# A token norm's sums, roots and reciprocals as nine columns instead of three packed strips

## The chip, the cores and the metric

The kernel runs on one core of a Trainium2 chip. The metric is the device time of one execution in microseconds (us), lower is better. TensorE (PE in the rows, its weight loads PEld) multiplies into PSUM, VectorE (DVE) and ScalarE (ACT) compute on tiles and move them out of PSUM, GpSimd (POOL) computes on SBUF only, and SyncE (SP) issues most of the transfers.

## The reference

One inference step of a trunk of two layers, for a prompt of 1024 tokens and for 8 samples of 8 tokens, with the same weights, all in float32. Layer 0 is a gated MLP, layer 1 ("the sparse layer") an attention in which a small indexer picks 256 keys for each query. Each layer is

```python
x <- x + W_out( mixer(rmsnorm(x, g)) * silu(z) )
x <- x + sigmoid(rmsnorm(x, g_pe) @ w_gate) * (p @ w_pe)

def rmsnorm(x, g):
    r = rsqrt(mean(x * x, axis=-1) + EPS)      # one number for each token
    return x * r * g
```

The work here is the first norm of layer 1: for each of 1088 tokens the sum of the squares of its 1024 features, a root, a reciprocal, and then the scaled `x` that goes into the projections of layer 1.

## The kernel before

`x` lies transposed in SBUF: `xT` is 128 partitions (features) by 8 tiles (k) by 1092 columns (64 sample tokens, 1024 prompt tokens, 4 columns of padding). All matrix products are made of three passes with float32r operands, a high and a low part of each side: `hhi`, `hlo` for the activations, `whi`, `wlo` for the weights. One unit is a product of a 1024 x 128 weight slab with all tokens; `full_unit` takes it in 8 steps over k, each of 9 matmuls with 364 columns (three column pieces, three passes), recorded at line 499, and each step waits for the low part of its tile k.

Each engine has its own program; semaphores alone join them. The order around the change is this:

- The end of layer 0's second half, the gate. For each feature tile TensorE makes a gate product (L499) and an embedding product (L2358); VectorE multiplies (L1599, L1603) and adds into `xT` (L1609); ScalarE makes the sigmoid (L1090); GpSimd squares the finished tile (L823) and adds it to `acc` (L824), for the first seven tiles.
- ScalarE squares the last tile into `sig` (`sparse_square`, L561).
- TensorE sums over the partitions (`strip_sums`, L570), by matmuls with ones: 32 columns of ones are the weights, 364 columns of squares move, and the three column pieces go to three strips of 32 PSUM partitions of bank 0. It does so for `acc`, waits for `sig`, and adds `sig`.
- ScalarE takes the root of 96 partitions by 364 columns (`strip_roots`, L576), VectorE the reciprocal (`strip_inverse`, L581).
- TensorE spreads the result back over all 128 partitions (`strip_spread`, L587): one row of ones is the weights, one row of reciprocals moves, from partitions 0, 32 and 64 into banks 5, 6, 7.
- Then the norm proper, for each k: VectorE scales `xT` by gain and reciprocal into `hfb` (L606), ScalarE rounds it to `hhi` (`norm_hi`, L592), VectorE subtracts for `hlo` (L612). There are two buffers of `hfb`. TensorE's first unit (U_IK, indexer keys) takes the tiles as they come.

ScalarE splits the next unit's weights (L482, `split_unit`) after the root, and GpSimd makes their low part (L487). SyncE waits for the count 2 of the norm's `sum` semaphore, loads the cosine and sine tables for the indexer (L727, L728) and goes on with weight slabs (L662).

A `Turn` gives each use of the norm the counts that its semaphores had before it; the turns are written out as tuples at the top of the kernel. For the sparse layer `sum` counts 2 in this kernel, one for the sums and one for the spread.

Of the kernel before, what the change touches and what calls it, by code (L numbers as in the profile page):

```python
# [22 lines left out]
ALU = mybir.AluOpType  # L23
ACT = mybir.ActivationFunctionType
AX = mybir.AxisListType

P = 128
D = 1024
KD = D // P
SEQ, DEC_B, DEC_T = 1024, 8, 8  # L30
NS = DEC_B * DEC_T
NT = NS + SEQ
TP = NT + 4
NC3 = TP // 3
# [17 lines left out]
BANK = 512  # L52
# [14 lines left out]
def tile_cols(j):  # L67

    return (0, NS) if j == 0 else (NS + CHUNK * (j - 1), CHUNK)
# [52 lines left out]
def hybrid_trunk(nc, x_prompt, x_sample, cache_k, cache_v, cache_ik, page_table, p_prompt, p_sample,  # L122
# [5 lines left out]
    with ctx:  # L128
# [23 lines left out]
        ident = fixed("ident", [P, P])  # L152
        ones = fixed("ones", [P, P])
        gains = fixed("gains", [P, NGAIN])
        gn = gains[:, 0:2 * KD].rearrange("p (l f) -> p l f", l=2)
# [3 lines left out]
        eps = fixed("eps", [P, 1])  # L159
        ss = fixed("ss", [P, 9])  # L160
        sv = fixed("sv", [P, 5])
        rv = fixed("rv", [P, 5])
        rx = fixed("rx", [P, 9])
# [5 lines left out]
        rbc = fixed("rbc", [P, TP])  # L169
# [52 lines left out]
        hhi = pl("hhi", [P, KD, TP], F32R)  # L222
        H1 = D0 + KD * TP * 4
        H2 = (END - KD * TP * 4) // 32 * 32
        hlo = nc.alloc_sbuf_tensor_at("hlo", [P, KD, TP], F32R, offset=H2)
# [11 lines left out]
        hfb = pl("hfb", [P, 2, TP])  # L237
# [87 lines left out]
        PS = ctx.enter_context(nc.psum_tensor("PS", [P, 8, BANK], F32))  # L325
        PSF = PS[:].rearrange("p b n -> p (b n)")
# [9 lines left out]
        def as3(ap):  # L336
# [9 lines left out]
        x_tr, x_sq, x_ev, x_rt, x_dg = (sem(n) for n in ("x_tr", "x_sq", "x_ev", "x_rt", "x_dg"))  # L346
# [5 lines left out]


        norm = {n: sem(f"norm_{n}") for n in ("sum", "rt", "hf", "hi", "lo")}
        turns = [Turn(norm, {"sum": (0, 2, 3, 6, 8)[t], "rt": (0, 0, 0, 3, 4)[t], "hf": KD * (0, 1, 2, 2, 3)[t],
                             "hi": KD * t, "lo": KD * t}) for t in range(5)]
        nA, nG, nB = turns[0:2], [turns[2], turns[4]], turns[3]

# [199 lines left out]
        def sparse_square(act):  # L558

            act.wait_ge(sG[0]["xup"], sG[0].at("xup", KD + 1))  # L560
            nc.scalar.activation(sig[:], xT[:, KD - 1, :], ACT.Square).then_inc(sq7, 1)  # L561

        def strip_sums(pe, s):

            pe.wait_ge(stat, 3)
            for part, squares in enumerate((acc, sig)):
                if part:
                    pe.wait_ge(sq7, 2)
                for c, (a, n) in enumerate(ALL_COLS):
                    mm = nc.tensor.matmul(PS[STRIP * c:STRIP * c + STRIP, 0, 0:n], ones[:, 0:STRIP], squares[:, a:a + n],  # L570
                                          start=part == 0, stop=part == 1)
            mm.then_inc(s["sum"], 1)

        def strip_roots(act, s):
            act.wait_ge(s["sum"], s.at("sum", 1))
            nc.scalar.activation(rbc[0:3 * STRIP, 0:NC3], PS[0:3 * STRIP, 0, 0:NC3], ACT.Sqrt, bias=eps[0:3 * STRIP],  # L576
                                 scale=1.0 / D).then_inc(s["rt"], 1)

        def strip_inverse(dve, s):
            dve.wait_ge(s["rt"], s.at("rt", 1))  # L580
            nc.vector.reciprocal(rbc[0:3 * STRIP, 0:NC3], rbc[0:3 * STRIP, 0:NC3]).then_inc(x_dg, 1)  # L581

        def strip_spread(pe, s):
            pe.wait_ge(x_dg, 4)
            for c, (a, n) in enumerate(ALL_COLS):
                row = slice(STRIP * c, STRIP * c + 1)
                mm = nc.tensor.matmul(PS[:, 5 + c, 0:n], ones[row, :], rbc[row, 0:n], start=True, stop=True)  # L587
            mm.then_inc(s["sum"], 1)

        def norm_hi(act, s, k, hi, hf):  # L590
            act.wait_ge(s["hf"], s.at("hf", k + 1))
            nc.scalar.activation(hi(k), hf(k), ACT.Copy).then_inc(s["hi"], 1)  # L592
# [22 lines left out]
        def norm_dve(dve, own, s, cols, *tile):  # L615
            a, n = cols[0][0], sum(c[1] for c in cols)
            if s in nA:
                dve.wait_ge(s["sum"], s.at("sum", 2))
            else:
                strip_inverse(dve, s)  # L620
                dve.wait_ge(s["sum"], s.at("sum", 2))
            for k in range(KD + 1):
                norm_tile(dve, s, k, a, n, *tile)

# [2 lines left out]
            return [(c0 + n // np_ * m, n // np_) for m in range(np_)]  # L627

        ALL_COLS = [(NC3 * c, NC3) for c in range(3)]
        STRIP = 32  # L630


        PIECES_P = [(kk, m, ((1, 2, 3), (0, 7, 3))[kk][m], NS * kk if m == 2 else 0, *(((NS, 512), (NS + 512, 512), (0, NS))[m]))
# [292 lines left out]
        def _(act):  # L926
            own = Tally(act, av)
# [44 lines left out]
            for g in range(2):  # L972
                c0, n, nch, has_s, np_ = GROUPS[g]
                h = n // np_
                s = sA[g]
# [134 lines left out]

            gate_act(0, False)

            sparse_square(act)
            strip_roots(act, nB)
            split_unit(U_IK + 1)
            for k in range(KD):
                norm_hi(act, nB, k, lambda k: hhi[:, k, :], lambda k: hfb[:, k % 2, :])

            def swap(dst, slot, size, scale, n=P):

# [272 lines left out]
            for f in range(KD):  # L1393
                act.wait_ge(oy["y"], f + 1)
                cols = slice(0, NS if f == 0 else TP)
# [10 lines left out]
        def _(dve):  # L1406
# [215 lines left out]
            def evac_out(f):  # L1622
# [3 lines left out]
                for m in range(3):  # L1626
# [4 lines left out]
                    else:  # L1631
# [1 line left out]

            gate_dve(0, False)

            norm_dve(dve, own, nB, ALL_COLS, lambda k: gn[:, 1, k:k + 1],
                     lambda k: hfb[:, k % 2, :], lambda k: hhi[:, k, :], lambda k: hlo[:, k, :], PS[:, 5:8, 0:NC3])

            def rotate(s, used, f, slot, dst, cs, sn, g):
                rotate_front(s, used, f, slot, cs, g)  # L1640
# [508 lines left out]
        def _(pe):  # L2149
# [258 lines left out]
                        within[i][1]()  # L2408
                mm.then_inc(w_used, 1)

            strip_sums(pe, nB)
            strip_spread(pe, nB)
            pe.wait_ge(sG[0]["t"], sG[0].at("t", KD + 1))
            def head_sum(n, rows, c):

# [391 lines left out]
```

## Time and profile before

| | us |
|---|---|
| median of 3 runs | 1891.24 |
| lowest, highest | 1890.42, 1893.8 |
| the profiled execution | 1889.96 |
| its span, first to last instruction | 1888.3 |
| TensorE busy | 1821.9 (96%) |
| VectorE busy | 889.5 (47%) |
| ScalarE busy | 796.0 (42%) |
| GpSimd busy | 617.8 (33%) |

All marks of time in the rows are microseconds from the start of the span. The profile's clock of TensorE (PEclk) is the granted share of 2.4 GHz, so 0.50 is 1.2 GHz. A float32 matmul that is not a transpose stands in the profile as two records, each with a weight load of its own; "x6" at the strip sums means three matmuls. The time of a record runs to the modelled end of a pipelined instruction, so records that follow each other overlap.

### The profile page before, as it was taken

The page shows a single profiled execution, that of the slowest core. Times are in us where ns is not written, and L with a number is a line of the kernel's source. Part 1 is how long each engine was busy: PE and PEld are TensorE (multiplying, and loading weights), DVE is VectorE, ACT ScalarE, POOL GpSimd, SP SyncE. Part 2 cuts the span into 40 slices and gives each one's busy share as a digit, 9 for nine tenths or more (in the row PEclk, how much of TensorE's full clock was granted, in tenths as well). Part 3 has the DMA queues.
Part 4 walks back from the last instruction along what each step waited for, and adds up shares of the span by engine and source line. Part 5 has one row for each costly group of instructions (what it writes and reads, how often), then busy time and mean ns, then how long its engine had stood idle before and what let it go on. Part 6 is the DMA issues. An engine that isn't in the chain of part 4 may idle for free.

```text
span 1888.3 us, 30009 instructions
## 1 busy us (share of the span) xinstructions
PE 1821.9 (96%) x10858; PEld 1616.9 (86%) x10858; DVE 889.5 (47%) x1647; ACT 796.0 (42%) x1186; POOL 617.8 (33%) x363
## 2 busy tenths in 40 slices
PE   8999999999999999999979989999999999899998
PEld 6889999999888888889969559999987776699997
DVE  3173333332124443142255877688778745612423
ACT  6243333222243333242235775477876554402211
POOL 4353333355444444644422131121121002254221
PEclk9999999999999999999989889999999999899999
DMA  5232222223333223331122110311242005521111
GB/s 195 78 90 78 78 67 78 78 78 89 91 99 89 83 84 89 90 112 45 33 106 80 31 57 23 93 44 58 92 130 63 1 1 207 197 92 43 46 58 48
DMA packets 203063, 150.81 MB, mean 80 GB/s; under 512 B 16626, under 2 KB 188450, under 8 KB 202594
## 3 DMA queue, kind: packets, MB, share of 16 engines
q1 hardware_dynamic: 188482, 127.88, 22.8%
q0 software_dynamic: 4272, 12.38, 2.0%
q10 hardware_dynamic: 10224, 9.46, 1.5%
q8 instruction: 48, 0.79, 0.2%
q14 instruction: 37, 0.30, 0.0%
HBM read 133.24 MB, written 16.43 MB: 79 GB/s over the span
## 4 chain that ended last, share of the span: by engine, by line
PE 88%; DVE 5%; issue 2%; ACT 2%; DMA 1%; POOL 1%; SPq 0%; ACTq 0%; DVEq 0%; POOLq 0%
PE PS L499 60%; PE PS L2217 10%; PE PS L2648 3%; PE PS L2618 3%; PE PS L2358 3%; PE PS L2483 2%; PE PS L2288 2%; PE PS L2664 1%; PE PS L2582 1%; DVE qT L2046 1%; DVE hlo L612 0%; POOL wlo L487 0%; PE PS L2504 0%; PE PS L2684 0%; PE PS L2636 0%
## 5 line engine op out<-in xcount | busy, mean ns | idle before, releaser
L487 POOL TENSOR_TENSOR wlo<-wraw,whi 128x1024 fp32r<-128x1024 f32 x177 | 434.8, 2457 | 752.1 <-ACT whi L482 751.6
L482 ACT ACTIVATE whi<-wraw 128x1024 fp32r<-128x1024 f32 x177 | 187.0, 1056 | 427.6 <-PE PS L499 314.0
L499 PE MATMUL PS<-hhi,whi 128*128 128x364 f32 x1176 | 270.3, 339 | 11.3 <-DVE hlo L612 7.1
L499 PE MATMUL PS<-hlo,whi 128*128 128x364 f32 x1176 | 262.5, 332 | 0.0
L499 PE MATMUL PS<-hhi,wlo 128*128 128x364 f32 x1176 | 261.0, 331 | 0.0
L499 PEld LDWEIGHTS PS<-hhi,whi 128*128 128x128 f32 x1176 | 204.2, 191 | 18.8 <-issue 12.0
L499 PE MATMUL PS<-hhi_g,whi 128*128 128x288 f32 (+1 forms) x768 | 214.5, 333 | 2.2 <-DVE v_raw L1488 1.8
L499 PE MATMUL PS<-hhi_g,wlo 128*128 128x288 f32 (+1 forms) x768 | 210.9, 329 | 0.0
L499 PE MATMUL PS<-hlo_g,whi 128*128 128x288 f32 (+1 forms) x768 | 210.5, 328 | 0.0
L499 PEld LDWEIGHTS PS<-hlo,whi 128*128 128x128 f32 x1176 | 206.9, 190 | 0.0
L499 PEld LDWEIGHTS PS<-hhi,wlo 128*128 128x128 f32 x1176 | 206.7, 190 | 0.0
L499 PEld LDWEIGHTS PS<-hhi_g,whi 128*128 128x128 f32 x768 | 130.2, 189 | 14.9 <-issue 2.3
L499 PEld LDWEIGHTS PS<-hhi_g,wlo 128*128 128x128 f32 x768 | 130.2, 188 | 11.7
L499 PEld LDWEIGHTS PS<-hlo_g,whi 128*128 128x128 f32 x768 | 130.8, 189 | 10.9
L1547 DVE TENSOR_TENSOR t2a<-PS,szt 128x576 f32<-128x576 f32 (+1 forms) x32 | 23.2, 725 | 206.2 <-PE PS L499 206.2
L499 PE MATMUL PS<-yhi,whi 128*128 128x288 f32 (+1 forms) x384 | 106.2, 331 | 0.0
L499 PE MATMUL PS<-ylo,whi 128*128 128x288 f32 (+1 forms) x384 | 105.2, 328 | 0.0
L499 PE MATMUL PS<-yhi,wlo 128*128 128x288 f32 (+1 forms) x384 | 104.9, 328 | 0.0
L1784 DVE TENSOR_SCALAR_CACHE_REDUCE acc<-sc,thr 128x384 bf16<-128x384 f32 (+1 forms) x124 | 100.7, 812 | 4.1
L1090 ACT ACTIVATE sig<-hfb 128x1092 f32<-128x1092 f32 x16 | 17.9, 1118 | 177.0 <-DVE hfb L1599 177.0
L1581 DVE TENSOR_TENSOR xT<-PS,xT 128x576 f32<-128x576 f32 (+1 forms) x16 | 11.6, 725 | 143.0 <-PE PS L499 143.0
L1171 ACT ACTIVATE acc<-sc,thr 128x896 bf16<-128x896 f32 (+1 forms) x62 | 67.8, 1093 | 20.9 <-DVE thr L1770 19.8
(421 smaller groups left out, 3106.6 us busy)
## 6 DMA issues: line engine op xcount, KB each, us to landing
wraw<-in_w_in_a_dram SPq DMA_DIRECT2D x96, 512.0 KB, 3.9
wraw<-in_w_out_a_dram SPq DMA_DIRECT2D x32, 512.0 KB, 4.0
wraw<-in_w_in_b_dram SPq DMA_DIRECT2D x25, 512.0 KB, 3.8
wraw<-in_w_pe_gate_dram SPq DMA_DIRECT2D x16, 512.0 KB, 4.0
kpg<-in_cache_k_dram SPq DMA_DIRECT2D x64, 128.0 KB, 2.9
vpg<-in_cache_v_dram POOLq DMA_DIRECT2D x48, 128.0 KB, 2.9
xs<-xT SPq DMA_DIRECT2D x1, 4368.0 KB, 12.6
xT<-xs SPq DMA_DIRECT2D x1, 4368.0 KB, 13.3
```

Of the source, the lines that this page charges most:

```text
L482: nc.scalar.activation(whi[par][:], wraw[par][:], ACT.Copy).then_inc(w_hi, 1)
L487: nc.gpsimd.tensor_tensor(wlo[par][:], wraw[par][:], whi[par][:].bitcast(F32), ALU.subtract).then_inc(w_lo, 1)
L499: mm = nc.tensor.matmul(o, w[par][:, k, :], r(k, c0, cn), start=first and i == 0 and n == 0, stop=last and i == KD - 1 and n == 2)
L1171: nc.scalar.activation(admp[:, 0:(b + 1) * P], area(b), ACT.Sign, bias=thr[:, b - 2:b - 1], scale=-1.0, accum_out=cnt[:, b - 2:b - 1]).the ...
L1547: nc.vector.tensor_tensor(t2a[:, 0:n].rearrange("p (b n) -> p b n", b=np_), PS[:, 2:2 + np_, 0:h], szt[:, 0:n].rearrange("p (b n) -> p b n ...
L1784: own.link(nc.vector.tensor_scalar(vdmp[:, 0:(b + 1) * P], area(b), thr[:, b - 2:b - 1], None, ALU.is_lt, ALU.add, accum_out=cnt[:, b - 2: ...
L2217: mm = nc.tensor.matmul(out, x, w, start=k == 0 and i == 0, stop=k == KD - 1 and i == len(products) - 1)
L2288: mm = nc.tensor.matmul(PS[:, 4, c * P:(c + 1) * P], vs[:, c * P:(c + 1) * P], wsT[:, bass.ds(i, 1), :].rearrange("p o t -> p (o t)"), sta ...
L2358: mm = nc.tensor.matmul(PS[:, EB + m, 0:NC3], w[:, k, :], r[:, k, m * NC3:(m + 1) * NC3], start=k == 0 and n == 0, stop=k == 1 and n == 2)
L2483: nc.tensor.matmul(PS[:, (m + 3) % 8, 0:n], iqT[p0:p0 + ID, h // 2, c0:c0 + P], ikT[p0:p0 + ID, NS + c * BANK:NS + c * BANK + n], start=Tr ...
L2618: mm = nc.tensor.matmul(PS[:, logit_bank(n) + a // BANK, 0:m], qT[:, h, c0:c0 + P], kT[:, h // REP, NS + a:NS + a + m], start=True, stop=True)
L2648: mm = nc.tensor.matmul(PS[:, 6 + i % 2, q * DH:(q + 1) * DH], PTs[:, k, q, :], vtok[:, 1 + k, g * DH:(g + 1) * DH], start=k == 0, stop=k ...
```

## The change

The sums are turned: the squares become the weights, 128 tokens (64 in the first tile) to a matmul, and one column of ones moves, so that each token's sum lands on that token's partition. Nine columns hold all 1088 tokens. The accumulated squares go to bank 0, those of the last tile to bank 1, and VectorE adds the two: it copies the first nine columns while the second half is still to come. ScalarE takes the roots of 64x1 and 128x8, VectorE the reciprocal of 128x9. TensorE turns the reciprocals back: the weights are one column repeated 128 times (a step of zero), the identity moves, and the result, one contiguous stretch of 1088 columns, begins 64 columns ahead of the end of bank 4. The norm's passes take 1088 columns instead of 1092. A root of one element per partition, on `eps`, is put ahead of `sparse_square`. The norm's `sum` now counts 3, and the turn after it begins at 9.

```diff
-        turns = [Turn(norm, {"sum": (0, 2, 3, 6, 8)[t], "rt": (0, 0, 0, 3, 4)[t], "hf": KD * (0, 1, 2, 2, 3)[t],
+        turns = [Turn(norm, {"sum": (0, 2, 3, 6, 9)[t], "rt": (0, 0, 0, 3, 4)[t], "hf": KD * (0, 1, 2, 2, 3)[t],
...
-        def strip_sums(pe, s):
+        def token_sums(pe, s):
 
             pe.wait_ge(stat, 3)
             for part, squares in enumerate((acc, sig)):
                 if part:
                     pe.wait_ge(sq7, 2)
-                for c, (a, n) in enumerate(ALL_COLS):
-                    mm = nc.tensor.matmul(PS[STRIP * c:STRIP * c + STRIP, 0, 0:n], ones[:, 0:STRIP], squares[:, a:a + n],
-                                          start=part == 0, stop=part == 1)
-            mm.then_inc(s["sum"], 1)
...
+                for j in range(9):
+                    c0, cn = tile_cols(j)
+                    mm = nc.tensor.matmul(PS[0:cn, part, j:j + 1], squares[:, c0:c0 + cn], ones[:, 0:1],
+                                          start=True, stop=True)
+                mm.then_inc(s["sum"], 1)
+
+        def token_roots(act, s):
+            act.wait_ge(x_dg, 4)
+            for rows, cols in ((NS, slice(0, 1)), (P, slice(1, 9))):
+                root = nc.scalar.activation(rx[0:rows, cols], rx[0:rows, cols], ACT.Sqrt, bias=eps[0:rows], scale=1.0 / D)
+            root.then_inc(s["rt"], 1)
+
+        def token_inverse(dve, own, s):
+            dve.wait_ge(s["sum"], s.at("sum", 1))
+            own.link(nc.vector.tensor_copy(rx[:], PS[:, 0, 0:9]))
+            dve.wait_ge(s["sum"], s.at("sum", 2))
+            nc.vector.tensor_tensor(rx[:], PS[:, 1, 0:9], rx[:], ALU.add).then_inc(x_dg, 1)
             dve.wait_ge(s["rt"], s.at("rt", 1))
-            nc.vector.reciprocal(rbc[0:3 * STRIP, 0:NC3], rbc[0:3 * STRIP, 0:NC3]).then_inc(x_dg, 1)
...
+            nc.vector.reciprocal(rx[:], rx[:]).then_inc(x_dg, 1)
+
+        RINV = 5 * BANK - NS
+        r_inv = PSF[:, RINV:RINV + NT].rearrange("p (b n) -> p b n", b=1)
+
+        def token_spread(pe, s):
+            pe.wait_ge(x_dg, 5)
+            for j in range(9):
+                c0, cn = tile_cols(j)
+                mm = nc.tensor.matmul(PSF[:, RINV + c0:RINV + c0 + cn], rx[0:cn, j:j + 1].broadcast_to((cn, P)),
+                                      ident[0:cn, 0:cn], start=True, stop=True)
             mm.then_inc(s["sum"], 1)
...
+            nc.scalar.activation(ss[:, 0:1], eps[:], ACT.Sqrt)
             sparse_square(act)
-            strip_roots(act, nB)
+            token_roots(act, nB)
             split_unit(U_IK + 1)
             for k in range(KD):
-                norm_hi(act, nB, k, lambda k: hhi[:, k, :], lambda k: hfb[:, k % 2, :])
+                norm_hi(act, nB, k, lambda k: hhi[:, k, 0:NT], lambda k: hfb[:, k % 2, 0:NT])
```

## Rows read from the trace of the kernel before

**Rows 1.** The page: the chain that ended last, by engine.
```profile
PE 88%; DVE 5%; issue 2%; ACT 2%; DMA 1%; POOL 1%; SPq 0%; ACTq 0%; DVEq 0%; POOLq 0%
```

**Rows 2.** Chain of waits from 954.9: start us, us, what.
```profile
954.92 1.35 PE PS L2358 x8
...
966.21 1.36 DVE hfb L606
...
985.64 7.74 PE PS L499 x45
```

**Rows 3.** Groups 955 to 989: xcount, busy us, mean ns, idle before.
```profile
L606 DVE SCALAR_TENSOR_TENSOR hfb<-xT,gains,PS 128x1092 f32<-128x1092 f32 x8 | 10.7, 1351 | 1.9 <-PE PS L587 1.7
L612 DVE TENSOR_TENSOR hlo<-hfb,hhi 128x1092 fp32r<-128x1092 f32 x8 | 10.3, 1290 | 0.0
```

**Rows 4.** Timeline 954 to 966: start us, us, engine, line, operation; [idle before, its releaser].
```profile
954.62 1.12 ACT L1090 ACTIVATE sig<-hfb 128x1092 f32<-128x1092 f32 x1 [11.85 <-DVE hfb L1599]
959.06 1.11 ACT L561 ACTIVATE sig<-xT 128x1092 f32<-128x1092 f32 x1 [3.32 <-DVE xT L1609]
960.19 1.28 ACT L576 ACT_TABLE_LOAD   x1
960.23 0.81 PE L570 MATMUL PS<-sig,ones 128*32 128x364 f32 x6 [3.23 <-ACT sig L561]
961.49 0.56 ACT L576 ACTIVATE rbc<-PS,eps 96x364 f32<-96x364 f32 x1
962.08 2.42 DVE L581 RECIPROCAL rbc<-rbc 96x364 f32<-96x364 f32 x1 [3.05 <-ACT rbc L576]
964.56 1.59 PE L587 MATMUL PS<-rbc,ones 1*128 1x364 f32 x6 [3.52 <-DVE rbc L581]
```

**Rows 5.** Windows: us, busy (x) of PE, PEld, DVE, ACT, POOL, granted clock, DMA share, GB/s.
```profile
960.00:961.70 1.70, 0.81 (x6) 0.15 (x6) 0.00 (x0) 1.67 (x3) 0.00 (x0) 1.00 0.00 0
961.80:964.50 2.70, 0.00 (x0) 0.00 (x0) 2.42 (x1) 1.19 (x2) 1.43 (x1) 0.50 0.00 0
970.10:975.40 5.30, 5.22 (x17) 5.25 (x18) 5.23 (x5) 2.24 (x2) 0.00 (x0) 0.50 0.83 228
```

**Rows 6.** Timeline and one window row: matmuls with 128-column weights, both clocks.
```profile
1200.55 0.80 PEld L2582 LDWEIGHTS PS<-ones,sqt 128*128 128x128 f32 x6
142.99 1.05 PE L2288 MATMUL PS<-wsT,vs 128*128 x8
1627.12 0.43 PE L2758 MATMUL PS<-rsb 128*128 128x64 f32 x2 [1.28 <-DVE rsb L2063]
1632.44 0.69 PE L2758 MATMUL PS<-rsb 128*128 128x64 f32 x2
1631.15 1.12 PE L2730 MATMUL PS<-ident,Ps 128*128 128x128 f32 x4
1631.10:1633.20 2.10, 2.02 (x11) 1.34 (x7) 0.33 (x2) 0.66 (x3) 0.00 (x0) 0.50 0.00 0
```

**Rows 7.** Small instructions: three of the timeline, one group of the lines by form.
```profile
131.32 0.30 ACT L1043 ACTIVATE rv<-sv,eps 128x5 f32<-128x5 f32 x1 [0.24 <-DVE sv L1518]
131.53 0.28 ACT L948 ACTIVATE rx<-ss,eps 128x4 f32<-128x4 f32 x1
27.53 0.19 DVE L1450 RECIPROCAL rx<-rx 128x5 f32<-128x5 f32 x1 [5.92 <-ACT rx L948]
L2067 DVE COPY qT<-PS 128x64 f32<-128x64 f32 x8 | 1.8, 221 | 2.5 <-PE PS L2758 2.4
```

**Rows 8.** Timeline of ScalarE, 988 to 1001.
```profile
988.98 1.06 ACT L482 ACTIVATE whi<-wraw 128x1024 fp32r<-128x1024 f32 x1 [3.45 <-PE PS L499]
989.95 1.06 ACT L1129 ACTIVATE sqt<-PS 64x1092 f32<-64x1092 f32 x1
...
999.06 1.02 ACT L1141 ACTIVATE rbc<-PS,eps 128x364 f32<-128x364 f32 x2
```

**Rows 9.** Timeline of SyncE's queue, 940 to 990.
```profile
966.20 0.36 SPq L727 DMA_DIRECT2D csI<-tcI  x1
```

More of the change, by code:

```diff
@@ L568, in strip_sums @@
                     pe.wait_ge(sq7, 2)
-                for c, (a, n) in enumerate(ALL_COLS):
-                    mm = nc.tensor.matmul(PS[STRIP * c:STRIP * c + STRIP, 0, 0:n], ones[:, 0:STRIP], squares[:, a:a + n],
-                                          start=part == 0, stop=part == 1)
-            mm.then_inc(s["sum"], 1)
[L574 to L577, printed above, removed]
@@ L579, in strip_inverse @@
-        def strip_inverse(dve, s):
-            dve.wait_ge(s["rt"], s.at("rt", 1))
-            nc.vector.reciprocal(rbc[0:3 * STRIP, 0:NC3], rbc[0:3 * STRIP, 0:NC3]).then_inc(x_dg, 1)
[L583 to L587, printed above, removed]
+                for j in range(9):
+                    c0, cn = tile_cols(j)
+                    mm = nc.tensor.matmul(PS[0:cn, part, j:j + 1], squares[:, c0:c0 + cn], ones[:, 0:1],
+                                          start=True, stop=True)
@@ L619, in norm_dve @@
             else:
-                strip_inverse(dve, s)
-                dve.wait_ge(s["sum"], s.at("sum", 2))
+                token_inverse(dve, own, s)
+                dve.wait_ge(s["sum"], s.at("sum", 3))
             for k in range(KD + 1):
@@ L629, in hybrid_trunk @@
         ALL_COLS = [(NC3 * c, NC3) for c in range(3)]
-        STRIP = 32
         PIECES_P = [(kk, m, ((1, 2, 3), (0, 7, 3))[kk][m], NS * kk if m == 2 else 0, *(((NS, 512), (NS + 512, 512), (0, NS))[m]))
@@ L1634, in _ @@
             gate_dve(0, False)
-            norm_dve(dve, own, nB, ALL_COLS, lambda k: gn[:, 1, k:k + 1],
-                     lambda k: hfb[:, k % 2, :], lambda k: hhi[:, k, :], lambda k: hlo[:, k, :], PS[:, 5:8, 0:NC3])
+            norm_dve(dve, own, nB, [(0, NT)], lambda k: gn[:, 1, k:k + 1], lambda k: hfb[:, k % 2, 0:NT],
+                     lambda k: hhi[:, k, 0:NT], lambda k: hlo[:, k, 0:NT], r_inv)
             def rotate(s, used, f, slot, dst, cs, sn, g):
@@ L2409, in full_unit @@
                 mm.then_inc(w_used, 1)
-            strip_sums(pe, nB)
-            strip_spread(pe, nB)
+            token_sums(pe, nB)
+            token_spread(pe, nB)
             pe.wait_ge(sG[0]["t"], sG[0].at("t", KD + 1))
```

## The prediction

> **What bounds the kernel now.** First the page: the chain that ended last lies 88% on TensorE [rows 1]. A change elsewhere pays only where TensorE waits, so I looked for the place in the chain of waits, merged in order of time [rows 2]. Look there for the stretch without TensorE: its last embedding product ends at 956.3, then come VectorE's two passes over the last feature tile (L1603, L1609), ScalarE's square (L561), and from 960.2 the norm's own chain: L576, L581, L587, and the first scaling pass L606 at 966.21. From the strip sums' start at 960.22 to that pass are 5.99 us. This is all that the change can touch: 0.32% of the run.
>
> Behind it VectorE sets the pace. Its passes L606 and L612 follow each other at (1.351 + 1.290) = 2.64 us a tile [rows 3], and eight tiles of that fill the time from 966.2 to 985.6 and a little over; TensorE, done with the nine matmuls of a tile in 9 x 7.74/45 = 1.55 us [rows 2] at full clock, waits for each low part. From 985.64 on the chain is TensorE's, 45 matmuls in one piece [rows 2]. So a shift of the first L606 by x moves all that follows by x, and I found no later wait that would swallow it: behind 985.64 every engine on the chain waits for work that moves along.
>
> **How the 5.99 us are made up** [rows 4]. Sums 0.81 (six records, three 32-column strips side by side: each record lasts 0.48, yet all six fit in 0.81), to 961.04. The root waits for its table: the load runs 960.19 to 961.47, so 0.45 us of it are on the path. Root 0.56 to 962.05, reciprocal 2.42 to 964.50, spread 1.59 to 966.15, and some 0.05 at each handover. The clock matters for what follows [rows 5]: TensorE stands still from 957.0 to 960.2, does the 0.81 of sums, and the granted clock is 1.00 up to 961.7 and 0.50 from 961.8 on, through the spread and until 975.4. That is 2.4 and then 1.2 GHz.
>
> **The change, part by part.**
>
> *Root table ahead.* A root on one column is put before the square. The load (1.28) and that instruction (about 0.3, as L948 [rows 7]) fit between the sigmoid's end at 955.74 and the square at 959.06 [rows 4]: 3.3 us of idle, 1.7 left over. Needed is that squares and copies run under the root's table: after the load of L576 there is no other, though ScalarE squares at 989.95 and takes roots at 999.06 [rows 8]. So there is no reload. It removes the 0.45 and no more, and even these only from the old order: with the new sums, which end after 961.5, a load in the old place would have been hidden.
>
> *Sums.* Instead of three packed pairs there are, for each half, nine matmuls with the squares as weights (128 columns) and a single moving column. Each is two records, as L2582, which is this very form. Its six weight loads take 0.80, or 0.12 to 0.13 each, and L2288's eight records with 128 moving columns take 1.05, that is 0.13 a record, or 0.11 if the last one's running out, some 0.16, is taken off [rows 6]. A lone pair (L2758, 64 columns) takes 0.43 at full clock and 0.69 at half; four single records at half take 1.12 (L2730), 0.28 each and, less the running out, some 0.22: the step doubles [rows 6]. So nine tiles take 0.43 + 8 x 0.22 = 2.2 us at full clock (18 x 0.13 = 2.3 at most), and with the step at 0.22 a record 0.69 + 8 x 0.44 = 4.2 at half (at most 18 x 0.28 = 5.0); the first tile has only 64 columns, so I take 4.1. The first half (of the accumulated squares) is issued at 956.2 and is over by 958.5, beside VectorE's passes and ahead of the square; nobody waits for it, nor for VectorE's copy of its nine columns at about 959.1, which lies beside the square. The second half waits for the square and is on the path. If the clock falls at 961.8 as in this trace, 1.58 of the 2.2 us are done, 29% are left, and they cost 1.2: the sums end at 963.0. Before they ended at 961.04.
>
> *Addition on VectorE, new on the path.* 128x9 out of PSUM. No row has it; L1450 (128x5, no PSUM) takes 0.19, L2067 (64 columns out of PSUM) 0.221 [rows 7]. I take 0.20, plus 0.05 handover: 963.25.
>
> *Roots.* Two small ones, 64x1 and 128x8, for one 96x364. L1043 and L948 begin 0.21 apart and last 0.30 and 0.28 [rows 7]: 0.50, with handover 0.54, to 963.8. L482 and POOL's L487 are queued behind them and go 2 us later; the unit they prepare is not wanted before TensorE has finished the one in work, some 22 us later (the next L482 is let go at 988.98 [rows 8]).
>
> *Reciprocal.* 128x9 like L1450's 128x5 at 0.19 [rows 7], with handover 0.23, to 964.0. Before: 2.44. This is the real gain, 2.2 us.
>
> *Spread.* Nine matmuls of two records, weights read from one column with zero step, 64 or 128 moving columns of the identity. 2.2 us at full clock, 4.1 at half; at half before, with three rows packed, 1.59 [rows 4]. TensorE has been even less busy than before, so I take half: 964.05 to 968.15, and L606 at 968.2.
>
> *Narrower passes.* 1088 for 1092 columns saves 16 x 1.32 x 4/1092 = 0.08 in all.
>
> *SyncE.* Its wait for the second count of the sums now ends with the sums and not with the spread, so the two table loads L727 and L728 go 3 us sooner than at 966.20 [rows 9]. They share no engine with the chain. Taken as nothing; from below nothing too, since nobody waits for them there.
>
> Sum: 2.8 (sums) + 0.25 + 0.54 + 0.23 + 4.2 = 8.0 for 5.99, less 0.08: **+2.0 us**. The profiled execution (1889.96, of which 1888.3 are the span) would go to 1892.0. It lies 1.3 below the median of the three runs; on the median I put 1891.24 + 2.0 = **1893.2**. About 0.2%, 3.8 us, is what a measurement of this kernel can tell from no change, so my forecast is "no change that can be told", on the slow side.
>
> **The price of a weight load.** A pair at half clock takes 0.69 for 0.43 at full [rows 6], though only 64 columns move: the load stretches with the clock. The Trainium skill, "TensorE: Matmul & The Clock Gate", section LDWEIGHTS, gives a load of P columns P/1.2 ns at either clock. By that, an estimate, the new sums would take 18 x 0.107 = 1.9 us and a little at half clock as at full, and the forecast would be some 0.6 lower, at +1.4. The trace does not agree, so it stays at +2.0.
>
> **Rivals.**
>
> *The clock stays up.* The 36 new records fill some 2.2 us before 958.5 and 2.2 us after 960.2, where TensorE stood still or was busy for 0.81. If that holds the clock at full until the spread is out, the stage is 2.2 + 0.25 + 0.54 + 0.23 + 2.3 = 5.5, that is 0.5 less than before: 1890.7. For it: TensorE stands still for less than 2 us before the sums instead of 3.2. Against: in [rows 5] the clock fell although 0.81 of packed 364-column work had just been done, and the new records move one column each. The same page of the Trainium skill, section "What's actually happening", says that activity releases the throttle and an idle stretch brings it back; it would be this rival if weight loads with one moving column are activity, which no row here shows.
>
> *The clock falls before the sums.* Its fall is not tied to an instruction of the kernel: 961.8 comes 4.8 us after the last dense product. Were it at 960 or before, the sums cost 4.1 and not 2.8: 9.3 for the stage, +3.3, 1894.5.
>
> *Slower for certain.* The spread's weights have zero step and come from a column written just before; no row has such a load. If its tiles do not overlap, each costs a lone pair at half clock, 0.69: 9 x 0.69 = 6.2 for 4.1, +4.1 in all, 1895.3. It decides from 0.65 us a tile. For it: nothing but the missing row; against: L2288 and L2582 overlap in all their runs, and the load of one column is no more to read.
>
> *The table comes back.* If the square throws the root's table out, one more load lies at 960.19 to 961.47, beside the sums: no cost, 1893.2 as well.
>
> *Faster by more than 3.8 us* would need the stage to shrink to 2.2 us, less than the sums alone. I know no mechanism.
>
> **How the numbers follow.** Forecast (clock falls during or right after the sums, half at the spread) 0.53; clock stays up 0.16; falls before the sums 0.20; spread without overlap 0.07; something unseen 0.04, half of it to each side. The bounds of the small terms are narrow (addition 0.17 to 0.3, roots 0.3 to 0.6), those of sums and spread are the two clocks. The range takes in both clock rivals with 0.7 us for the medians' own scatter: 1890.0 to 1895.4. Slower by over 0.2% (above 1895.0): the 0.07, the 0.02 and a bit of the cold case's scatter, 0.12. Faster 0.03. Within 0.2%: 0.85.
>
> **What would show it.** The table load between the sigmoid and the square, none after it. VectorE's add beginning at 2.2 to 4.1 us after the sums' start; the reciprocal near 0.2; the spread near 4.1 with the granted clock at 0.50, or near 2.2 at 1.00, which settles the rivals. From the sums' start to the first L606 8.0 us, and all later marks shifted by the same 2 us. I am wrong if that stretch is under 6 or over 9.5, if a reload appears on the path, or if the shift at 985.6 is not the shift at the end.

## The result, and the profile after

| | before | changed |
|---|---|---|
| median, us | 1891.72 | 1897.75 |
| lowest to highest, us (8 runs each) | 1890.42 to 1893.8 | 1894.63 to 1901.43 |
| ratio, 95% interval | | 1.0032 [1.0021, 1.0043] |
| the profiled execution, us | 1889.96 | 1897.13 |
| its span, us | 1888.3 | 1895.5 |
| granted clock, mean | 0.983 | 0.982 |
| TensorE busy, us | 1821.9 | 1833.4 |

The change costs 6.0 us in the medians, 7.2 in the two spans. The forecast was +2.0 and its range ended at 1895.4. The page after, the chain by engine (the answer to [rows 1]):

```profile
PE 89%; DVE 5%; issue 2%; ACT 2%; POOL 1%; DMA 0%; ACTq 0%; DVEq 0%; SPq 0%; POOLq 0%
```

**The place of the change.** Timeline of the changed kernel, 954 to 970, the answer to [rows 4]: start us, us, engine, line, operation; [idle before, its releaser].

```profile
955.55 1.28 ACT L1122 ACT_TABLE_LOAD   x1
955.97 2.07 PEld L571 LDWEIGHTS PS<-ones,acc 128*64 128x64 f32 x18 [0.23 <-issue]
955.97 2.15 PE L571 MATMUL PS<-ones,acc 128*64 128x1 f32 x18
956.84 0.20 ACT L1122 ACTIVATE ss<-eps 128x1 f32<-128x1 f32 x1
958.73 0.16 DVE L583 COPY rx<-PS 128x9 f32<-128x9 f32 x1
...
960.01 3.79 PEld L571 LDWEIGHTS PS<-ones,sig 128*64 128x64 f32 x18 [1.97 <-ACT sig L561]
960.01 3.87 PE L571 MATMUL PS<-ones,sig 128*64 128x1 f32 x18 [1.89 <-ACT sig L561]
963.91 0.36 SPq L736 DMA_DIRECT2D csI<-tcI  x1
963.99 0.17 DVE L585 TENSOR_TENSOR rx<-PS,rx 128x9 f32<-128x9 f32 x1 [5.10 <-PE PS L571]
964.19 0.49 ACT L578 ACTIVATE rx<-rx,eps 64x1 f32<-64x1 f32 x2 [4.24 <-DVE rx L585]
964.71 0.21 DVE L587 RECIPROCAL rx<-rx 128x9 f32<-128x9 f32 x1 [0.55 <-ACT rx L578]
964.98 4.22 PE L596 MATMUL PS<-ident,rx 64*128 64x64 f32 x18 [1.10 <-DVE rx L587]
969.24 1.35 DVE L616 SCALAR_TENSOR_TENSOR hfb<-xT,gains,PS 128x1088 f32<-128x1088 f32 x1 [4.32 <-PE PS L596]
```

The same 18 records take 2.15 us in the first half and 3.87 in the second. From the sums' start at 960.01 to the first scaling pass at 969.24 are 9.23 us; before they were 966.21 less 960.23, 5.98 [rows 4]. So +3.25 for the stretch. The pass itself moved by 3.03, since the stretch began 0.22 earlier. TensorE's long piece, which began at 985.64, now begins at 988.62 (the chain of waits), 2.98 later; the end of the span is 7.2 later. The prediction had named that difference as a sign that it is wrong.

Windows of the changed kernel, with the columns of [rows 5]: us, busy (x) of PE, PEld, DVE, ACT, POOL, granted clock, DMA share, GB/s.

```profile
956.00:958.50 2.50, 2.12 (x19) 2.02 (x18) 2.28 (x2) 1.03 (x2) 0.00 (x0) 1.00 0.00 0
958.80:960.00 1.20, 0.00 (x0) 0.00 (x0) 0.09 (x2) 1.11 (x1) 0.00 (x0) 0.50 0.00 0
960.00:964.00 4.00, 3.87 (x18) 3.77 (x18) 0.01 (x1) 0.00 (x0) 0.00 (x0) 0.50 0.00 0
...
1047.00:1129.00 82.00, 72.91 (x310) 39.09 (x310) 68.83 (x155) 67.19 (x126) 24.32 (x9) 0.90 0.19 48
1232.00:1242.00 10.00, 10.00 (x39) 10.00 (x38) 4.36 (x8) 2.71 (x6) 1.63 (x1) 0.50 0.20 52
```

The clock (2.4 GHz at 1.00, 1.2 at 0.50) is down by 958.8. In the trace of before it was still 1.00 between 960.0 and 961.7 [rows 5].

**The rest of the run.** Behind the change, inside each unit of the query projection, TensorE also makes three small groups of float32 matmuls that sum ScalarE's squares for the heads (L2582, one moving column each); these are "the head sums". A table of marks, from the rows of both kernels:

| mark | before | changed | shift |
|---|---|---|---|
| first scaling pass | 966.21 | 969.24 | +3.03 |
| SyncE issues a weight slab (512 KB) | 1194.11 | 1195.90 | +1.79 |
| ScalarE splits that slab (L482) | 1200.47 | 1202.94 | +2.47 |
| first head sums inside a projection | 1227.72 | 1230.21 | +2.49 |
| the fourth such block | 1241.99 | 1249.13 | +7.14 |
| end of the span | 1888.3 | 1895.5 | +7.2 |

Two things happen far behind the change. Between 966 and 1194, 1.2 us come back, and in the windows the low clock is rarer there: 0.90 between 1047 and 1129, where before had 0.85 (first row below). Then 0.7 and 4.65 us are lost between 1194 and 1249. The same views of the kernel before: windows,

```profile
1045.00:1127.00 82.00, 73.67 (x308) 40.97 (x309) 68.52 (x153) 65.97 (x125) 24.32 (x9) 0.85 0.18 48
1231.80:1241.80 10.00, 10.00 (x64) 9.88 (x62) 8.22 (x18) 6.20 (x9) 1.18 (x1) 1.00 0.19 52
```

its timeline (SyncE's queue, ScalarE, TensorE; the slab is the first of the four),

```profile
1194.11 21.24 SPq L662 DMA_DIRECT2D wraw<-in_w_in_b_dram  x4
1200.47 1.06 ACT L482 ACTIVATE whi<-wraw 128x1024 fp32r<-128x1024 f32 x1 [4.48 <-DMA wraw<-in_w_in_b_dram]
1227.72 0.81 PE L2582 MATMUL PS<-ones,sqt 128*64 128x1 f32 x6 [0.82 <-ACT swp L1123]
```

and its chain of waits behind the head sums (start us, us, what):

```profile
1230.71 1.61 PE PS L499 x9
...
1232.88 9.11 PE PS L499 x54
1241.99 0.74 PE PS L2582 x6
```

The changed kernel, timeline and then chain:

```profile
1195.90 11.12 SPq L671 DMA_DIRECT2D wraw<-in_w_in_b_dram  x3
1202.94 1.06 ACT L482 ACTIVATE whi<-wraw 128x1024 fp32r<-128x1024 f32 x1 [5.14 <-DMA wraw<-in_w_in_b_dram]
1230.21 0.81 PE L2592 MATMUL PS<-ones,sqt 128*64 128x1 f32 x6 [1.49 <-ACT swp L1133]
```

```profile
1231.01 2.25 PE PS L499 x9
...
1234.34 2.94 PE PS L499 x9
...
1238.35 10.78 PE PS L499 x54
1249.13 0.74 PE PS L2592 x6
```

The slab takes 7.04 us from issue to split and not 6.36. ScalarE's work behind it, down to the squares that the head sums read, is that much later, so TensorE, which keeps going until it has nothing else, stands still for 1.49 us before the sums and not 0.82. Then the clock falls: nine L499 records with 364 columns take 2.94 us where they took 1.61, and so it stays for 10 us. TensorE was dense before the gap; after it come six records that move one column and nine wide ones, and the fall is among these nine (2.25 us for 1.61; the windows have 1.00 up to 1231.4 and 0.50 from 1231.8).

What made the slab take longer? The trace has 16 KB transfers on an instruction queue, q8. That they fetch TensorE's program is read from e5 below: matmuls added for TensorE alone bring one more of them (49 for 48) and move this one 5 us ahead. The DMA view of before has none between 1194.1 and 1199.2, and this between 1199.4 and 1199.8, 5.4 us behind the slab's issue (queue: transfers, MB, share of 16 engines):

```profile
q8 instruction: 1, 0.02, 17.0%
```

In the changed kernel the one such transfer begins some 0.4 us behind the issue, at 1196.3, while the slab's packets are being moved (the view from 1195.9 to 1196.6):

```profile
q8 instruction: 1, 0.02, 8.6%
```

The page counts 49 of them for 48, and 10894 TensorE records for 10858: 36 matmul records (with their weight loads 72 instructions) more, so every later fetch falls on another instant. That is the theory that the experiments test against "a delay of 3 us is simply worth more than 3".

### The profile page after: what moved, and what is told of

Read it like the earlier page. It is cut to its first block, busy times and chain, and to the rows that moved or that the text cites. A ratio compares the mean times of both kernels' runs of the same rounds, so it can differ in the third digit from the quotient of the medians.

```text
span 1895.5 us, 30086 instructions
## 1 busy us (share of the span) xinstructions
PE 1833.4 (97%) x10894; PEld 1628.7 (86%) x10894; DVE 888.2 (47%) x1649; ACT 796.4 (42%) x1188; POOL 618.2 (33%) x363
## 4 chain that ended last, share of the span: by engine, by line
PE 89%; DVE 5%; issue 2%; ACT 2%; POOL 1%; DMA 0%; ACTq 0%; DVEq 0%; SPq 0%; POOLq 0%
PE PS L499 60%; PE PS L2227 10%; PE PS L2658 3%; PE PS L2628 3%; PE PS L2368 3%; PE PS L2493 2%; PE PS L2298 2%; PE PS L2674 1%; PE PS L2592 1%; DVE qT L2056 1%; DVE hlo L622 0%; POOL wlo L487 0%; PE PS L2694 0%; PE PS L2646 0%; PE PS L2514 0%
## 5 line engine op out<-in xcount | busy, mean ns | idle before, releaser
L482 ACT ACTIVATE whi<-wraw 128x1024 fp32r<-128x1024 f32 x177 | 186.9, 1056 | 428.1 <-PE PS L499 314.4
L499 PE MATMUL PS<-hhi,whi 128*128 128x364 f32 x1176 | 271.6, 340 | 10.9 <-DVE hlo L622 6.7
L499 PE MATMUL PS<-hlo,whi 128*128 128x364 f32 x1176 | 263.0, 332 | 0.0
L499 PE MATMUL PS<-hhi,wlo 128*128 128x364 f32 x1176 | 261.9, 331 | 0.0
L499 PEld LDWEIGHTS PS<-hhi,whi 128*128 128x128 f32 x1176 | 205.4, 192 | 18.3 <-issue 11.9
L499 PE MATMUL PS<-hhi_g,whi 128*128 128x288 f32 (+1 forms) x768 | 214.1, 333 | 2.2 <-DVE v_raw L1498 1.8
L499 PE MATMUL PS<-hhi_g,wlo 128*128 128x288 f32 (+1 forms) x768 | 210.9, 329 | 0.0
L499 PE MATMUL PS<-hlo_g,whi 128*128 128x288 f32 (+1 forms) x768 | 210.3, 328 | 0.0
L499 PEld LDWEIGHTS PS<-hhi,wlo 128*128 128x128 f32 x1176 | 207.5, 191 | 0.0
L499 PEld LDWEIGHTS PS<-hlo,whi 128*128 128x128 f32 x1176 | 207.5, 191 | 0.0
L499 PEld LDWEIGHTS PS<-hhi_g,whi 128*128 128x128 f32 x768 | 130.0, 189 | 14.9 <-issue 2.3
L499 PEld LDWEIGHTS PS<-hhi_g,wlo 128*128 128x128 f32 x768 | 130.2, 188 | 11.8
L499 PEld LDWEIGHTS PS<-hlo_g,whi 128*128 128x128 f32 x768 | 130.5, 188 | 11.0
L499 PE MATMUL PS<-ylo,whi 128*128 128x288 f32 (+1 forms) x384 | 105.6, 329 | 0.0
L499 PE MATMUL PS<-yhi,whi 128*128 128x288 f32 (+1 forms) x384 | 105.3, 328 | 0.0
L499 PE MATMUL PS<-yhi,wlo 128*128 128x288 f32 (+1 forms) x384 | 105.1, 327 | 0.0
```

Source lines behind the costliest of these rows:

```text
L482: nc.scalar.activation(whi[par][:], wraw[par][:], ACT.Copy).then_inc(w_hi, 1)
L499: mm = nc.tensor.matmul(o, w[par][:, k, :], r(k, c0, cn), start=first and i == 0 and n == 0, stop=last and i == KD - 1 and n == 2)
```

## The experiments

Each was measured against the kernel before on the same chip; "us" is a median.

**e1: the table alone.** In `before`, ahead of `sparse_square(act)`:

```diff
+            nc.scalar.activation(ss[:, 0:1], eps[:], ACT.Sqrt)
```

> The kernel before with one edit: the root on one column ahead of the last square; the packed strips stay. Theory (the stage is what its parts add up to): the load leaves the path, 0.45 us less from the strip sums to the first scaling pass (5.99 to 5.54), and the run is 0.4 us faster, which cannot be told from no change. Rival (moving the table load causes part of the 6 us lost, by a reload or a wait): the run is at least 1 us slower than before.

Measured: 1891.85 against 1891.43, ratio 1.0 [0.9991, 1.0009]. The stretch takes 965.91 less 960.32 = 5.59 us, 0.4 less than before, with no second load: the 0.4 is gained in the stretch and is too small to be seen in the whole.

**e2: a delay and nothing else.** In `strip_inverse` of `before`, one reciprocal more:

```diff
             dve.wait_ge(s["rt"], s.at("rt", 1))
+            nc.vector.reciprocal(hfb[0:3 * STRIP, 1, 0:490], acc[0:3 * STRIP, 0:490])
```

> The kernel before with nothing but a delay: VectorE makes one more reciprocal of 96x490 into a buffer nobody reads, ahead of the real one, by the rate of the 96x364 one (2.42 us) 3.3 us. It brings the stage to 9.2 us, as the changed kernel has it in its profile. Theory A (only 3.2 us of the loss belong to the stage; the rest comes later in the run from any shift of this size): about as slow as the changed kernel, 5 to 7 us over before, and its times scatter as widely. Theory B (the loss beyond the stage belongs to something else in the change): +3.3 us, with the small scatter of before. The profile should show in theory A the clock down at about 1232 as in the changed kernel.

Measured: 1894.56, +3.1, ratio 1.0016 [1.0007, 1.0025], for a stretch of 971.04 less 961.98 = 9.06, +3.1. At the later place, its timeline and then a window:

```profile
1232.55 0.81 PE L2583 MATMUL PS<-ones,sqt 128*64 128x1 f32 x6 [0.86 <-ACT swp L1124]
```

```profile
1234.00:1244.00 10.00, 10.00 (x66) 10.00 (x65) 8.60 (x15) 6.21 (x9) 1.99 (x1) 1.00 0.19 52
```

The gap is the old one and the clock stays at 1.00. In the medians a delay as long as the change's costs its own length; "more than its length" falls. The profiled execution is the slowest of the 11 (1897.16, span 1895.6): of its 7.3 us over before, 1.8 lie ahead of the stretch, 3.1 in it and 2.5 behind the head sums at 1232.55, so single executions differ by a few us at places that no edit touched.

**e3 and e4: the head sums one step later**, in the changed kernel and in the one before, so that TensorE has a step of wide matmuls more to do while ScalarE is late:

```diff
-                return inside(*((k, q_sums, f, part) for part, k in enumerate((5, 6, 7))))
+                return inside((6, q_sums, f, 0), (7, q_rest, f))
```

(`q_rest` is parts 1 and 2 in one.)

> The changed kernel with the head sums of the query units moved from steps 5, 6 and 7 of the unit behind to 6, 7 and 7, so that TensorE asks for ScalarE's square later (near 1229 of the span). Theory (after the stage, the second loss is TensorE's idle time of 1.5 us there, with single-column sums behind it, in which the clock falls for 10 us at a price of about 4.3): the granted clock stays at full there and the run is 2 to 4 us faster than the changed kernel, 3 us over before, with less scatter. Rival (the second loss is spread over the run or elsewhere): as the changed kernel, +6.

> The kernel before with the same move of the head sums. Theory: it has 0.8 us of idle time there and no fall of the clock, so it gains at most 1 us and cannot be told from before. Rival (the later sums themselves are worth something, or cost something, wherever the clock stands): a shift of 2 us or more either way, and then the move in the changed kernel must be read against it.

Measured: e3 1891.73 (1891.05 to 1892.72), ratio 1.0002 [0.9993, 1.0011]; e4 1890.99, ratio 0.9996 [0.9987, 1.0005]. In e3 the stretch of the change still takes 969.29 less 960.08 = 9.21 us and the slab 7.10, but there is no gap, and the window where the changed kernel was at half reads 1.00:

```profile
1234.00:1244.00 10.00, 10.00 (x61) 10.00 (x61) 9.29 (x18) 7.29 (x9) 1.92 (x1) 1.00 0.20 52
```

So moving small groups 260 us behind the change takes away nearly the whole loss (+6.0 becomes +0.3), and the same edit gives the kernel before 0.4. That is more than the 2 to 4 us expected and more than the 4.65 lost at the gap. Beside e4, the change costs 0.7 in the medians (1891.73 less 1890.99) though its stretch is 3.2 longer; the two profiled spans differ by 2.9 (1890.4 and 1887.5). Where the medians get the other 2.5 us back is not shown: the clock in the 82 us from 1045 or 1047 on is 0.90 in both profiles.

**e5 and e6: instructions and nothing else.** 18 one-column matmuls (36 records), behind a wait that they don't lengthen: in `before` ahead of the strips' spread, where TensorE idles, and in the changed kernel behind its spread.

```diff
+        def pad(n):
+            for _ in range(n):
+                nc.tensor.matmul(PS[0:32, 7, 0:1], ones[:, 0:32], ones[:, 0:1], start=True, stop=True)
```

> The kernel before with 18 tiny float32 matmuls (32 weight columns, one moving column) ahead of the strip spread, where TensorE waits 3.5 us anyway: as many TensorE instructions more as the change adds, 36 records, and nothing of its work. Theory F (the second loss comes from where TensorE's instruction fetch falls: 72 instructions further on, its 16 KB transfer at 1199.5 of before is made at about 1195, amid the stores and the weight slab that ScalarE waits for; the slab lands 0.65 us later, TensorE's idle gap near 1227 goes from 0.8 to 1.5 us, and the clock falls there for 10 us): this kernel loses the second part without the first, 3 to 4 us over before, with the clock down after about 1229. Rival (the second loss needs the stage's shift, or the two transfers that SyncE issues earlier): no loss, within 0.5 us of before.

> The changed kernel with the same 18 tiny matmuls behind its spread, where TensorE waits 4 us for the first low part. Theory F: the fetch moves another 4 to 5 us ahead, to before the weight slab, so the slab lands in time again and only the stage's 3 us are left: 1894.5, with little scatter. Rival: as the changed kernel, 1897 to 1898.

Measured: e5 1893.61 (1891.61 to 1898.45) against 1891.34, ratio 1.0016 [1.0007, 1.0025]. The stretch is unchanged (5.98), and yet, in its timeline:

```profile
1201.05 1.06 ACT L482 ACTIVATE whi<-wraw 128x1024 fp32r<-128x1024 f32 x1 [5.21 <-DMA wraw<-in_w_in_b_dram]
1228.29 0.81 PE L2587 MATMUL PS<-ones,sqt 128*64 128x1 f32 x6 [1.53 <-ACT swp L1128]
```

The slab was issued at 1193.94, so 7.11 to the split, and the gap is the changed kernel's, 1.53. In this execution (1891.74, near the lowest) the clock did not fall; two of the 11 took 1898.2 and more, as long as the changed kernel. e6: 1893.58, ratio 1.0013 [1.0004, 1.0022], +2.2 where the changed kernel has +6.0, though it has more instructions. Its stretch was 0.9 shorter (968.18 less 959.87, the clock fell later in it), its slab took 6.50, its gap was 0.94,

```profile
1228.46 0.81 PE L2597 MATMUL PS<-ones,sqt 128*64 128x1 f32 x6 [0.94 <-ACT swp L1137]
```

and between the slab's issue at 1194.70 and its split at 1201.20 the DMA view has no q8 transfer. So the late slab and the wider gap come by added instructions without the norm's new work, and go by adding still more. Both runs lie short of what was expected in size: e5 lost 2.3 and not 3 to 4, and of e6's 3.8 us under the changed kernel 0.9 lie in its shorter stretch.

**e11: the same 18 matmuls in `before`, with the sums later** as in e4.

> The kernel before with the 18 tiny matmuls and with the head sums moved later. Theory F (the 18 matmuls cost time only by the idle gap near 1227, through the slab that lands late): with no gap there, nothing is lost; as the kernel before with later sums alone, 0 to 1 us under before, although the slab still lands 0.7 us later. Rival (more TensorE instructions cost time elsewhere): about 2 us over before, as with the 18 matmuls alone.

Measured: 1890.68, ratio 0.9997 [0.9988, 1.0006]. The slab is still late (1193.95 to 1201.07, 7.12), there is no gap, and nothing is lost (e5's interval began at 1.0007, this one ends at 1.0006): e5's price is paid at the gap.

**e7 and e10: is it the clock in the norm's own stretch?** Wide matmuls on data at hand, into an unused bank. e7 has 8 between the halves of the sums and 4 ahead of the spread; e10 has one between every two tiles of the first half (8), two in the second and 4 ahead of the spread.

```diff
+                nc.tensor.matmul(PS[:, 7, :], whi[0][:, 0, :], whi[0][:, 0:4, :].rearrange("p k c -> p (k c)"),
+                                 start=True, stop=True)
```

> The changed kernel with 8 dense matmuls of 512 columns between the two halves of the sums and 4 between the sums and the spread, into a bank nobody reads, in time that TensorE has idle. Theory (the stage is 3.2 us longer because sums and spread run at 1.2 GHz): at 2.4 GHz the sums take 2.2 and the spread 2.2 instead of 3.9 and 4.2, the stage 5.5 instead of 9.2; the run 3 to 3.7 us under the changed kernel, and half of that if the clock falls in between all the same. Rival (turned sums and spread are slow at any clock): stage over 8 us, run as the changed kernel or later by what the fillers push.

> The changed kernel with dense matmuls laid between the tiles: eight through the first half of the sums, two in the second half (0.43 us of price on the path), four ahead of the spread. In the first try they stood behind the first half, after 2.1 us without dense work, and the clock had fallen before they could act. Theory (sums and spread are slow by the clock alone): it stays at 2.4 GHz to the spread, sums 2.2 + 0.4, spread 2.2, stage about 6.0 for 9.2, run 3 us under the changed kernel of this call. Rival: stage over 8.

e7: 1896.82, ratio 1.0022 [1.0013, 1.0031]. It failed as a test: the clock fell at about 960.8 all the same (0.69 in the mean from 960 to 962), the eight took 3.01 us, most of them at half, and held the sums up, which then took 3.87 again. e10: 1897.44, ratio 1.0031 [1.0020, 1.0041]. Its timeline has the second half of the sums in three pieces; the windows are one of the sums and one of the spread:

```profile
961.72 0.81 PE L579 MATMUL PS<-ones,sig 128*64 128x1 f32 x6
962.71 0.72 PE L579 MATMUL PS<-ones,sig 128*128 128x1 f32 x6
963.61 0.85 PE L579 MATMUL PS<-ones,sig 128*128 128x1 f32 x6
...
966.31 4.40 PE L605 MATMUL PS<-ident,rx 64*128 64x64 f32 x18
```

```profile
962.00:964.00 2.00, 2.00 (x17) 1.92 (x17) 0.00 (x0) 0.00 (x0) 0.00 (x0) 1.00 0.03 8
968.00:970.00 2.00, 2.00 (x11) 2.00 (x11) 0.00 (x0) 0.00 (x0) 0.63 (x1) 0.50 1.04 341
```

With wide matmuls between its tiles the clock stays at 1.00 to 964, and the sums take 0.81 + 0.72 + 0.85 = 2.4 us where they took 3.87. So the clock alone made them slow. The fillers ahead of the spread ran at half, and so did the spread: its time at full clock was seen in no run. The expected 6.0 us of stretch did not come: with the fillers in the way it is 970.74 less 961.72 = 9.02, and the run gained nothing. Neither profile has a fall of the clock behind the head sums; the first scaling pass alone is 5.9 us (e7) and 4.5 us (e10) later than before, and their spans are 6.3 and 4.4 longer.

**e8 and e12: four strips.** The old form, with four strips of 272 columns for three of 364, root table ahead, and 1088 columns in the passes; e12 with the later sums as well.

```diff
+        NQ = NT // 4
+        QUARTERS = [(NQ * c, NQ) for c in range(4)]
...
-            nc.vector.reciprocal(rbc[0:3 * STRIP, 0:NC3], rbc[0:3 * STRIP, 0:NC3]).then_inc(x_dg, 1)
+            nc.vector.reciprocal(rbc[:, 0:NQ], rbc[:, 0:NQ]).then_inc(x_dg, 1)
```

> A version that should beat both: the packed strips of before, but four of 272 columns for three of 364, and the root's table ahead. Sums 0.65 for 0.81, root 0.45 for 0.56, reciprocal (272/364) x 2.42 = 1.8, spread 1.3 for 1.59 at half clock, and the 0.45 of the table: a stage of 4.4 for 5.99. Theory: 1.6 us under before, 1889.8. Rival (six more record pairs of TensorE move its instruction fetch a little and bring a loss elsewhere): stage as said, but the run no faster than before.

> Four strips, the table ahead and the later head sums together. If the two gains add, 0.4 us under the four strips alone (which had 3.7 us on before), so 4 us under before; if four strips had already escaped the gap, no difference from them. A value above before would mean that the gain of the four strips was luck of the clock.

Measured: e8 1887.63 (1885.6 to 1890.55) against 1891.34, ratio 0.9980 [0.9971, 0.9989]; e12 1887.47 against 1891.66, ratio 0.9982 [0.9973, 0.9991]. Both beat the kernel before, and with it the changed one; the later sums add nothing to four strips. e8's timeline:

```profile
960.52 0.67 PE L570 MATMUL PS<-sig,ones 128*32 128x272 f32 x8 [3.37 <-ACT sig L561]
...
961.78 1.85 DVE L581 RECIPROCAL rbc<-rbc 128x272 f32<-128x272 f32 x1 [2.45 <-ACT rbc L576]
963.69 1.29 PE L587 MATMUL PS<-rbc,ones 1*128 1x272 f32 x8 [2.50 <-DVE rbc L581]
965.04 2.61 DVE L606 SCALAR_TENSOR_TENSOR hfb<-xT,gains,PS 128x1088 f32<-128x1088 f32 x2 [1.41 <-PE PS L587]
```

4.52 us, 1.46 less than before. The medians gained 3.7, and 1.6 were expected, so 2.2 of it are not explained by this stretch. The profiles show where time was gained behind it: from the first scaling pass to the slab's issue are 224.33 us (e12 224.35) where before has 227.90, with a granted clock of 0.94 from 1045 to 1127 for 0.85. In e8's profile 1.4 of these 3.6 us are lost again later. Why the clock is low less often there was not tested, so this part of the gain may hang on how this kernel's waits fall, and not on the strips as such.

**e9: the changed kernel once more.**

> The changed kernel itself once more, beside the three others on one chip, as their measure. All theories: 5 to 7 us over before. Its profile tells whether the clock's fall near 1232 comes back: where the stage stays at 8.3 to 9.3 us and the fall is missing, the span should be near 1891 and not 1895.

Measured: 1899.82 (1896.84 to 1901.26, 5 runs), ratio 1.0043 [1.0029, 1.0057]. The slab took 7.09 us (1198.14 to 1205.23), and the gap and the fall are there again, in timeline and window:

```profile
1232.48 0.81 PE L2592 MATMUL PS<-ones,sqt 128*64 128x1 f32 x6 [1.53 <-ACT swp L1133]
```

```profile
1234.00:1244.00 10.00, 10.00 (x39) 10.00 (x38) 4.37 (x8) 2.99 (x6) 1.91 (x1) 0.50 0.19 52
```

## Why the prediction was wrong

*The step that failed* is "a shift of the first L606 by x moves all that follows by x, and I found no later wait that would swallow it", and with it a sum made of the stretch alone. The runs showed a shift of 3.03 at the first L606 and of 7.2 at the end. I looked for a wait that would swallow the shift and not for one that the added instructions would lengthen. The later wait for the slab grew by 0.7, the gap before the head sums doubled, and the clock fell for 10 us: 2.49 to 7.14 in the marks, 4.65 of the 7.2. e3 takes nearly all of the 6.0 us of the medians away without touching the norm. I counted the 36 added records by the time they take in the stretch, and put at nothing, without a reason, what they could change elsewhere; e5 adds as many, hidden and without the norm's new work, and it lost 2.3 us.

*A rival came true beside it.* The clock fell before the sums, priced at a stretch of 9.3 and 1894.5; measured 9.23. I took the fall at 961.8 over from the trace of before, where TensorE had done 0.81 us of packed 364-column work at 956 and again at 960. The change takes just that work away. I used the single columns only against the rival in which the clock stays up. That error is 1.2 us (9.23 for 8.0), nearly all of it in the sums, 3.87 for 2.8; with it alone the time would have been 1891.72 + 3.2 = 1894.9 by e2's rate, inside the range.

*The small terms held.* Predicted and measured: addition 0.20 and 0.17; roots 0.50 and 0.49; reciprocal 0.19 and 0.21; sums at half 4.1 and 3.87; spread at half 4.1 and 4.22. The first half of the sums 2.2 and 2.15. The table load lies between the sigmoid and the square, and none came back. SyncE's table loads went early (963.91, before 966.20 [rows 9]) and cost nothing seen. "Slower for certain" and "the clock stays up" fell: the spread's tiles overlap (18 records in 4.22 us), and the clock was at half in sums and spread.

*The weight load's price.* 18 loads take 2.07 us in the first half of the sums at clock 1.00 and 3.79 in the second at 0.50. The Trainium skill, "TensorE: Matmul & The Clock Gate", section LDWEIGHTS, gives P/1.2 ns for P columns and names no clock; that it holds at either clock was the prediction's reading. By it, an estimate, 18 loads take at most 1.9 us. The rows at 1.00 are near this, those at 0.50 are twice as long, so one price for both clocks is not what they show; the estimate of +1.4, which left the spread's 18 loads as they were, would have been further off.

*What stays open.* That the fetch amid the slab's packets is what delays the slab: with the fetch 0.5 us behind the issue the slab takes 7.04 to 7.12 us (five profiles: the changed kernel, e3, e5, e9, e11), with it 5.2 us or more behind, or none, 6.35 to 6.50 (before, e1, e2, e4, e6, e8, e12), and 1.0 ahead 6.64 (e7, e10). The pairing has no exception in 14 profiles, but no run moved the fetch alone, and the view doesn't show a packet of the slab that waited for it. Why the clock falls after a gap of 1.5 us in some executions and not in all (e5) stays open too; a gap of 0.8 to 0.9 saw none in five profiles (before, e1, e2, e6, e8), one of 1.2 none in two (e7, e10). The 1.2 us given back between 966 and 1194 can't be put down to the change: from the first scaling pass to the slab's issue the changed kernel takes 226.66 us and before 227.90 (e1, e2, e5 and e11 227.85 to 227.87), but e4, whose program is that of before up to there, takes 226.44, also with a clock of 0.90.

## What to carry to other kernels

Before pricing added instructions by their time, list the places where TensorE stands still for about a microsecond with single-column work behind, and ask what feeds each. Here 0.7 us more of such a gap went with a clock fall that cost 4.65 us, and the cure was to put the small work one dense step later. When dense work is replaced by narrow work, don't take the clock of the old trace for the new stretch. And where several rows are each computed on a few partitions, one strip more (four of 272 for three of 364) shortened every step of this chain at once, and with the root's table ahead it beat turning the layout.

## What was not expected of the hardware

- The granted clock was down by 958.8, 0.7 us after 2.15 us of gapless single-column records; with 512-column matmuls laid between the tiles it was 1.00 until 964 (e10).
- 36 records placed where they hide (e5) cost 2.3 us, with a slab 0.7 us late some 230 us behind them, and nothing once the gap there was gone (e11). That the slab was late by a 16 KB program fetch fits all profiles and is not shown.
- A reciprocal of 96x364 takes 2.42 us [rows 4] and one of 128x272 1.85; a spread of six records of 364 columns 1.59 [rows 4], eight of 272 1.29, 18 with 128 or fewer at half clock 4.22.
